# A hybrid decoder step in fp32: the attention branch as seven block products per tile pair, with its gated rows added by DMA

## What is computed

```
h   = RMSNorm(x);  proj = h @ w_in -> q, k, v, B, C, u, gate_a, gate_b
A   = sliding-window attention (window 128, 16 query heads, 2 key heads, sinks, rotary)
b   = B * dwconv3(C * u)
merged = sigmoid(ga + bias) * (A @ w_attn_branch) + sigmoid(gb + bias) * (b @ w_conv_branch)
x  += RMSNorm(merged @ w_o)
f   = (gelu(dwconv3(a) + bias) * g) @ w_ffn_down,  a, g = RMSNorm(x) @ w_ffn_up;  x += RMSNorm(f)
x  += sigmoid(x @ w_ple_gate) * (p @ w_ple)
```

## Time and profile before

| | |
|---|---|
| median of 3 runs | 2649.91 us (2649.46 to 2651.39) |
| span of the profiled execution | 2648.5 us; no time of its own is listed beside it |
| granted TensorE clock | 1.000 over the span |
| PE busy | 2641.1 us |
| DVE busy, ACT busy, POOL busy | 2221.4, 1386.6, 189.5 us |

### The profile page before, as it was taken

How to read it: one execution, slowest core, us unless ns; L and a number is a source line. 1 busy time by engine, 2 the same in 40 slices (tenths; PEclk the granted TensorE clock), 3 DMA queues, 4 the chain that set the end, 5 groups by cost and what they waited for, 6 DMA issues and landing times.

```text
span 2648.5 us, 55450 instructions
## 1 busy us (share of the span) xinstructions
PE 2641.1 (100%) x20949; PEld 2582.9 (98%) x20949; DVE 2221.4 (84%) x3913; ACT 1386.6 (52%) x2533; POOL 189.5 (7%) x289
## 2 busy tenths in 40 slices
PE   9999999999999999999999999999999999999999
PEld 8999999999999999999999999999999999999899
DVE  7988888888896687898888888888888768789987
ACT  6544555555563255655555555555555453445454
POOL 0221000000010000000000000000000000000000
PEclk9999999999999999999999999999999999999999
DMA  6676334333484355655566555665569575565774
GB/s 229 187 209 184 134 117 142 133 124 117 158 262 160 131 165 158 247 174 161 169 206 186 181 162 167 191 198 175 158 188 306 158 239 173 162 207 162 251 265 151
DMA packets 160028, 479.65 MB, mean 181 GB/s; under 512 B 17177, under 2 KB 51361, under 8 KB 156480
## 3 DMA queue, kind: packets, MB, share of 16 engines
q1 hardware_dynamic: 128752, 370.81, 39.7%
q0 software_dynamic: 30960, 106.59, 18.0%
q10 hardware_dynamic: 144, 0.15, 0.0%
HBM read 420.63 MB, written 55.71 MB: 180 GB/s over the span
## 4 chain that ended last, share of the span: by engine, by line
PE 97%; DVE 2%; issue 0%; ACT 0%; DMA 0%; SPq 0%; DVEq 0%; ACTq 0%
PE pair L1208 78%; PE pair L1173 6%; PE pair L1328 3%; PE pair L1306 3%; PE pair L1111 2%; PE pair L935 1%; PE pair L1285 1%; PE pair L1133 1%; PE pair L987 1%; PE pair L1008 1%; DVE v_lo L1977 0%; DVE lo L2328 0%; PE pair L997 0%; DMA s_raw<-in_sstream 0%; PE pair L1068 0%
## 5 line engine op out<-in xcount | busy, mean ns | idle before, releaser
L1208 PE MATMUL pair<-o_hi,v_hi 128*128 128x260 f32 x5840 | 1657.6, 284 | 1.2 <-DVE v_lo L1977 0.8
L1208 PE MATMUL pair<-o_hi,v_lo 128*128 128x260 f32 x5840 | 1650.1, 283 | 0.0
L1404 ACT ACTIVATE v_hi<-s_raw 128x512 fp32r<-128x512 f32 (+1 forms) x1368 | 852.1, 626 | 931.3 <-PE pair L1208 795.3
L1208 PE MATMUL pair<-lo,v_hi 128*128 128x260 f32 x4172 | 1179.3, 283 | 0.0
L1977 DVE TENSOR_TENSOR v_lo<-s_raw,v_hi 128x512 fp32r<-128x512 f32 (+1 forms) x1288 | 874.0, 681 | 301.1 <-ACT v_hi L1404 265.1
L1208 PEld LDWEIGHTS pair<-o_hi,v_hi 128*128 128x128 f32 x5840 | 1099.0, 188 | 14.9 <-issue 11.9
L1208 PEld LDWEIGHTS pair<-o_hi,v_lo 128*128 128x128 f32 x5840 | 1100.8, 188 | 0.0
L1208 PEld LDWEIGHTS pair<-lo,v_hi 128*128 128x128 f32 x4172 | 784.8, 188 | 0.2
L1208 PE MATMUL pair<-lo_E,v_hi 128*128 128x260 f32 x834 | 236.2, 283 | 0.0
L1404 ACT ACTIVATE v_hi<-s_one 128x512 fp32r<-128x512 f32 (+1 forms) x220 | 137.1, 626 | 189.1 <-PE pair L1208 164.5
L1208 PE MATMUL pair<-lo_A,v_hi 128*128 128x260 f32 x834 | 235.3, 282 | 0.0
(11 more groups left out here) (287 smaller groups left out, 2494.7 us busy)
## 6 DMA issues: line engine op xcount, KB each, us to landing
s_raw<-in_sstream SPq DMA_DIRECT2D x468, 512.0 KB, 4.9
s_one<-in_sstream POOLq DMA_DIRECT2D x168, 512.0 KB, 5.4
raw<-f_scr SPq DMA_DIRECT2D x12, 1040.0 KB, 7.6
s_raw<-in_sstream SPq DMA_DIRECT2D x32, 384.0 KB, 4.0
g_scr<-d_h SPq DMA_DIRECT2D x16, 520.0 KB, 2.7
g_in<-g_scr SPq DMA_DIRECT2D x32, 260.0 KB, 2.8
x_scr<-y_sb SPq DMA_DIRECT2D x8, 1040.0 KB, 5.3
s_one<-in_sstream POOLq DMA_DIRECT2D x16, 384.0 KB, 4.8
```

The lines of the kernel that those rows point to most:

```text
L1208: mm = pe.matmul(out, wt[:, slot, kk * P:kk * P + P], r[:, k, :], start=j in (0, 1, 3) and k == 0 and n == 0, stop=k == nk - 1 and n == 2, ...
L1404: nc.scalar.activation(v_hi[:, n % 4, 0:width], src, ACT.Copy, scale=0.5 if halved(u) else 1.0).then_inc(v_hi_rdy, 1)
```

## The change

1. The attention branch becomes eight units `U_AT` to `U_AT + 7` of the same form as the conv units. `conv_unit` becomes `branch_unit` for both. The weight is cut as the conv branch's is (`conv_pairs`).
2. The attention steps are reordered (`step_of`): head group outside, block inside. The output of a group's four steps gathers in `aw`. When a group is complete, DVE makes its four differences (`attention_form`), and POOL stores the seven forms to `af_scr` (two transfers). For group 3 DVE makes them in unit `U_BR + 1`. SP loads forms 0 to 3 in unit `U_BR + 2`, 4 to 6 in unit `U_AT - 1`. ACT and DVE split them (`af_high`, `af_low`).
3. The attention results land in `d_h[u % 2]`, are gated there (`attention_gated`), and POOL adds them to `x_tile` with accumulating transfers (`merge`), except the last two rows, which DVE adds (`add_last`). ACT's first copy of unit u waits until the rows of unit u - 2 are added.
4. Waits on `merged_ready` become `rows_merged`. The first sum of `U_O` is now made by transfers too, and pieces of `t1`, `t2`, `t3`, `s3` move into the last attention units.

```diff
-                blk, w = n // 4, n % 4
+                blk, w = step_of(n)
...
             def attention_out(n):
+                blk, w = step_of(n)
+                if blk == 0:
+                    act.wait_ge(as_rdy, 1)
+                    if w:
+                        act.wait_ge(af_stored, 32 * w)
+                    nc.scalar.activation(aw[:, :, TP:T], as_st[:, 2 * w:2 * w + 2, :], ACT.Copy)
...
             def branch_unit(u):
...
                     if j == 0:
+                        if u in (U_AT, U_AT + 1):
+                            act.wait_ge(h_stored[u % 2], 16 * stores_before(U_BR + u % 2))
+                        elif u > U_AT:
+                            act.wait_ge(merged_in, 32 * (u - U_AT - 1))
+                        copied(u, 0, d11, r1_out)
...
-                    if U_BR + 1 < u < U_O - 2 and j in (2, 4):
-                        br_high(rows_split(u) + j // 4)
+                    if U_BR + 3 <= u < U_AT - 1 and j == 2:
+                        af_high(u - U_BR - 3)
+                    if u == U_AT - 1 and j >= 4:
+                        af_high(j)
...
+            def attention_gated(m):
+
+                u = U_AT + m // 2
...
+                row = d_h[u % 2][:, m % 2, :]
+                dve.scalar_tensor_tensor(out=row, in0=g_in[m % 4][:, :], scalar=1.0, in1=row,
+                                         op0=ALU.add, op1=ALU.mult).then_inc(br_free, 1)
...
-                    if u > U_BR and j in (1, 6):
-                        conv_gated(m - 2 + j // 6)
+                    if u > U_BR and j in (1, 5 if u > U_AT else 6):
+                        branch_gated(u - 1, j // 5)
...
-                    if U_BR + 1 < u < U_O - 2 and j in (3, 5):
-                        br_low(rows_split(u) + j // 5)
+                    if u == U_BR + 1 and j in (3, 4, 5, 6):
+                        attention_form(3, {3: 1, 4: 2, 5: 4, 6: 6}[j])
+                    if U_BR + 3 <= u < U_AT - 1 and j == 3:
+                        af_low(u - U_BR - 3)
+                    if u == U_AT - 1 and j == 6:
+                        af_low(4)
+                    if u == U_AT and j in (1, 2):
+                        af_low(4 + j)
...
+                    if u == U_O - 1 and j == 5:
+                        rows_merged(dve, KH + 4)
+                        t2(1, 0)
+                    if u == U_O - 1 and j == 6:
+                        t3(1, 0)
...
+            for m in (KD - 2, KD - 1):
+                attention_gated(m)
+                add_last(m)
+            rows_merged(dve, KD)
...
-                pool.wait_ge(a_rdy, n + 1)
...
+                if n % 4 == 3:
+                    w = n // 4
+                    if w == 3:
+                        add_conv_sum(U_BR + 2)
+                    pool.wait_ge(af_rdy, 4 * w + 4)
+                    pool.dma_start(af_scr[0:4, :, w, :].rearrange("n p t -> p n t"),
+                                   aw.rearrange("p r (h t) -> p (r h) t", h=2)).then_inc(af_stored, 16)
+                    pool.dma_start(af_scr[4:7, :, w, :].rearrange("n p t -> p n t"),
+                                   (last_forms if w == 3 else cv_forms)[:, 0:3, :]).then_inc(af_stored, 16)
+
+            def merge(u):
+
+                i = u - U_AT
+                if i:
+                    pool.wait_ge(merged_in, 32 * i)
+                for n in range(2):
+                    pool.wait_ge(br_free, KD + 2 * i + n + 1)
+                    pool.dma_start(x_tile(2 * i + n), two(d_h[u % 2][:, n, :]), accum_op=ALU.add)\
+                        .then_inc(merged_in, 16)
 
-            for u in range(U_BR + 2, U_O):
+            for u in range(U_BR + 3, U_O):
                 add_conv_sum(u)
+                if u - 3 >= U_AT:
+                    merge(u - 3)
+            merge(U_O - 3)
+            add_first_sum(U_O)
+            merge(U_O - 2)
```

More of the change, by code:

```diff
@@ L26 @@
 U_BR = 32
-U_O = U_BR + KD // 2
+U_AT = U_BR + KD // 2
+U_O = U_AT + KD // 2
 U_UP = U_O + KD // 2
@@ L36 @@
 PLAIN = (0, U_UP, U_GATE)
+CONV_H = 14 * U_BR + 7 * (U_AT - U_BR)
 BR_H = 14 * U_BR + 7 * (U_O - U_BR)
-PLE_H = BR_H + 2 * KD + 14 * (U_UP - U_O)
+PLE_H = BR_H + 14 * (U_UP - U_O)
 NPH = 8
 R_CONV = U_BR + 1
-R_BR = R_CONV + KD // 4
-R_PLE = R_BR + KD // 4 + KD // 2
+R_O = R_CONV + KD // 2
+R_PLE = R_O + KD // 2
 NR = R_PLE + 1 + U_END - U_UP
@@ L77, in h_of @@
         return 14 * U_BR + 7 * (u - U_BR) + j
[L78 removed]
+    return BR_H + 14 * (u - U_O) + 2 * j + h + (NPH if u >= U_UP else 0)
 def r_of(u):
@@ L85, in r_of @@
         return R_CONV + (u - U_BR) // 2
-    return R_BR + KD // 4 + u - U_O + (1 if u >= U_UP else 0)
+    return R_O + u - U_O + (1 if u >= U_UP else 0)
 def unit_of(r):
@@ L223, in build @@
         pT_sb = sub("pT_sb", [P, 2, 4, BLK])
-        a_st = [sub(f"a_st{i}", [P, 2, BLK]) for i in range(2)]
+        aw = sub("aw", [P, 2, T])
         assert o[0] <= r_g + KD * XB
@@ L360, in by_dma @@
             return (2 <= u < U_CONV + 6 or u == U_SIG + 1 or U_BR <= u < U_O
-                    or u > U_O and u not in PLAIN)
+                    or u >= U_O and u not in PLAIN)
         def sums_of(u, h):
@@ L741, in _ @@
             for u in range(U_BR, U_O):
+                if u == U_BR + 2:
+                    sp.wait_ge(af_stored, 32 * 4)
+                    af_load(0, 1, 2, 3)
+                if u == U_AT - 1:
+                    for j in range(3):
+                        product_done(u, j)
+                        af_load(4 + j)
                 if u % 2:
@@ L2726, in conv_gated, with add_last, branch_gated, branch_unit @@
                                          op0=ALU.add, op1=ALU.mult).then_inc(br_free, 1)
-            def conv_unit(u):
+            def attention_gated(m):
+                u = U_AT + m // 2
+                for e in ((c11_out, c12_out), (c22_out, c21_out))[m % 2]:
+                    dve.wait_ge(e, u + 1)
+                dve.wait_ge(g_rd[m % 4], 16 * (KD // 4 + m // 4 + 1))
+                row = d_h[u % 2][:, m % 2, :]
+                dve.scalar_tensor_tensor(out=row, in0=g_in[m % 4][:, :], scalar=1.0, in1=row,
+                                         op0=ALU.add, op1=ALU.mult).then_inc(br_free, 1)
+            def add_last(m):
+                dve.wait_ge(br_free, KD + m + 1)
+                dve.tensor_tensor(x_tile(m), x_tile(m), two(d_h[(U_O - 1) % 2][:, m % 2, :]), ALU.add)\
+                   .then_inc(merged_ready, 1)
+            def branch_gated(u, n):
+                if u < U_AT:
+                    conv_gated(2 * (u - U_BR) + n)
+                else:
+                    attention_gated(2 * (u - U_AT) + n)
+            def branch_unit(u):
                 n, h = s_of(u, 0, u % 2), u % 2
                 m = 2 * (u - U_BR)
+                if u < U_AT:
+                    d11, d12, d22 = x_tile(m)[:, 0, :], x_tile(m)[:, 1, :], x_tile(m + 1)[:, 1, :]
+                else:
+                    d = d_h[u % 2]
+                    d11, d12, d22 = d[:, 0, 0:HALF], d[:, 0, HALF:T], d[:, 1, HALF:T]
                 for j in range(7):
-                    d11, d12, d22 = x_tile(m)[:, 0, :], x_tile(m)[:, 1, :], x_tile(m + 1)[:, 1, :]
                     if j in (3, 4, 5) and (u > U_BR or j > 4):
@@ new lines, in branch_unit @@
+                    if u == U_AT + 6 and j == 6:
+                        rows_merged(dve, KH)
+                        t1(1, 1)
+                    if u == U_O - 1 and j == 2:
+                        both_halves(s3, U_O)
+                    if u == U_O - 1 and j == 5:
[3 more added lines that the diff above has]
+                        t3(1, 0)
+            for u in range(U_BR, U_O):
+                branch_unit(u)
```

252 lines of the change are left out of this document (103 added, 149 removed).

## The result

The changed kernel takes 2694.5 us (median; 2693.6 to 2695.9), the kernel before 2649.8 us in the same comparison. The ratio is 1.0167, with a 95% interval of 1.0153 to 1.0181: 44.6 us slower. The prediction said slower, 2667.0 us (its 2667.1, laid on the 2649.8 of this comparison), with a range that ended at 2683. The direction was right, the size was too small by 27.5 us and the range did not hold it.

The account below looks back on a forecast made before the run. PE, busy 2641.1 of 2648.5 us, was taken as the bound. Terms -11.5 + 2.2 + 5.7 + 1.0 + 2.5 + 15.3 + 2.0 = +17.2 us, added to 2649.9, gave 2667.1 us; range 2649 to 2683.

Parts of the forecast that it names:

- The matmuls, -11.5: Attention branch: 768 matmuls become 672, 96 fewer at 0.1195 us each, -11.5 us, called the sure part.
- Splits of forms 0 to 3, +2.2: Units U_BR + 3 to U_BR + 6: DVE's 1040-column splits delay the addition releasing product 6, +2.2 us (1.5 to 2.8).
- POOL's late sum, +5.7 and +1.0: U_BR + 3: POOL's sum queued behind group 3's form stores makes PE wait, +5.7 us; chained next sums, +1.0.
- Around `U_AT`, +2.5: Unit U_AT: DVE's low parts of forms 4 to 6 delay the addition before product 6, +2.5 us (0.5 to 3.5).
- The merge, +15.3: Units U_AT + 2 to U_AT + 7: PE stalls L - 1.25 us before product 2, 2.55 us six times, +15.3.
- The landing L: Time for POOL's accumulating row transfer to land, taken as 3.8 us from the accumulating 256 KB load's 3.8, 5.0, 8.0.
- The rival with L of 5.0 and more: Queues collide with SP's 2 MB loads; POOL's late sum costs 9.1: +28 us, 2678 us; chance 0.15 (above 2675).
- Every new wait of PE is added in full: Whole kernel: PE is always busy and nothing else is late, so each new PE wait adds its full length.
- The end of the branch, +2.0: Output projection's first unit: longer DVE chain to s2(U_O) stalls PE 1.0 us, then delays product 6; +2.0 (0.5 to 3.5).
- no cost, but near: First sum of U_O: transfers issued some 12 us before use against about 11 for both landings; no cost.

Follow-up runs that it names:

- the additions left out: Kernel with all rows added by DVE, three buffers and low parts of all forms moved, now without the additions of rows 0 to 13: 2644.2 us.
- the filling: Changed kernel plus dummy matmuls ahead of product 2 in U_AT + 2 to U_AT + 7 and product 1 in U_BR + 3: 2691.6 us.
- The removal of the merges: Changed kernel with U_BR + 3's sum queued before the last forms' wait and all rows added by DVE: 2650.9 us (two buffers), 2650.2 (three).
- the third buffer: Changed kernel with three buffers for gated rows, so ACT waits for the merge of unit u - 3, not u - 2: 2668.7 us.
- both: Changed kernel with the third buffer and with U_BR + 3's sum queued on POOL ahead of the last forms' wait: 2662.7 us.
- the later low part: Kernel with all rows added by DVE and three buffers, low parts of forms 0 to 3 moved from product 3 to product 5: 2649.8 us.
- the early sum: Changed kernel with the sum for U_BR + 3 queued on POOL ahead of the wait for the last forms: 2684.8 us.

## Why the prediction was wrong

**The matmuls, -11.5.** The branch line has 1344 at 0.1195 us. Right as work; it is not worth 11.5 us of time. Even with the additions left out, 6.0 us reached the end: 3.6 us went in the branches, and 2.5 in the projection's first unit, which hangs on DVE's work behind the last product.

**Splits of forms 0 to 3, +2.2.** The four units are 10.79 us long, 0.75 over 10.04: 3.0, less the 0.7 of before, +2.3. Right; the profile lists it as waits of 0.44 us and the rest as their edges.

**POOL's late sum, +5.7 and +1.0.** The queue and its order were right: 763.18 for a predicted 763.75, 774.9 for 774.3 at the landing, a wait of 6.5 us. With the edges and the lower clock behind the wait it is 8.5 us against 6.7.

**Around `U_AT`, +2.5.** DVE made PE wait 1.9 us at the predicted instruction. The prediction had ACT's copy of product 0 in time there; it was not, and PE stood 0.6 us for it, and 0.5 us more before product 5. That is 3.1 us of waits, within the range, and 3.9 with their edges, just outside.

**The merge, +15.3.** This is the step that failed, together with the price of the lower clock below. Its mechanism was right, in place, in number (six units) and in the formula. The landing L was mis-sized: 3.8 us was the shortest landing of the nearest row in size and kind, chosen because the source lay in SBUF. The transfers on the chain took 5.3 us in the mean and 4.17 at the least. The middle of that very row, 5.0, would have given +22.5, and 22.9 was measured, 7.6 us more than forecast. A plain copy from SBUF to SBUF took 4.0 us in the mean too, so nearness of the path bought little. The rival with L of 5.0 and more was the one nearest to what came, and its 2678 was still too low.

**What was missing.** "Every new wait of PE is added in full" took the matmuls behind a wait at the full clock. No term and no rival priced what PE's idle time does to its own clock. It is 13.7 us in the stage, 12.0 of them behind the merges and 1.6 behind the late sum. With the merge's waits mis-sized by 7.6 us and their edges of 2.2, this is 23.5 of the 27.5 us by which the forecast was low; `U_AT` and the end of the branch add 2.6. With the merge's waits alone put right, the sum would be +24.8 us, inside the stated range; with the lower clock too it is +38.5, outside. This is not exact: part of the slower work ran while the next merge was on its way, as the filling showed. The removal of the merges is the better number: 33.9 us for waits of 25.5.

**The end of the branch, +2.0.** The output projection's first unit is 3.2 us longer in the kernel after, 1.8 and 0.7 us of it as PE's waits. Within its range.

The merge also did something that the prediction denied: transfers ahead of `s_one`'s load in POOL's queue were called "no cost, but near". In the changed kernel this is hidden behind slower PE; when PE is faster, as with the third buffer, it shows as waits of 3.4 us (third buffer) and 8.0 us (both) ahead of the product that reads `s_one`.

It stays open how the 33.9 us divide exactly between waiting and clock, since each moves the other, and why a wait of 1.9 us before product 6 of `U_AT` had 13 to 15 slow matmuls behind it in four kernels (without the addition in the transfer, with DVE's additions and two or three buffers, with the later low part), and none in the changed kernel and the ones with the early sum, the third buffer, both and the filling.

## What to carry to other kernels

Price a wait that repeats by the middle of the nearest row's landing times, not by its shortest, and ask what stands behind the transfer in the same queue. Where TensorE has been busy without a pause, a new wait of some microseconds costs more than its length: here 33.9 us for 25.5 us of waiting. And before counting on fewer matmuls, see whether the other engines have time to spare and what hangs on the last product: here DVE was busy for 66.8 of 70 us with the adds on it, and even without them half of the saved 11.5 us did not reach the end.

## What the runs showed of the hardware

- The granted clock fell to 0.50 with each of the waits of 2.75 to 6.5 us in the changed kernel, and 15 to 26 matmuls of 260 columns then started 0.217 us apart, not 0.12. Waits of 0.4 to 0.6 us had none behind them. Those of 1.8 and 1.9 us had 13 to 15 in five places of these runs and none in several others; one of 2.99 us in the kernel with the early sum and one of 3.40 us in the one with a third buffer had none.
- A wait also costs PE its overlap: 0.16 us at its start and 0.10 to 0.26 at its end, so that waits of 0.44 us made units 0.75 us longer.
- Copying a row of 266 KB from SBUF to SBUF on POOL's queue took 3.0, 4.8 and 9.8 us (least, middle, most); adding it took 4.0, 5.4 and 11.2 us, and POOL's issue 1184 instead of 727 ns. With less waiting between them the adding ones took 4.2, 7.2 and 13.0 us.
- One such transfer in a unit of 10 us, five in all, landed in 6.1, 6.7 and 7.2 us (least, middle, most) beside the loads and held up nothing.
